# Layer norm sums by halving additions, and modulation pieces moved from the output product to the feed-forward

## The reference, cut to what matters

```python
def layer_norm(x, g, b):
    mu = jnp.mean(xf, axis=-1, keepdims=True)
    var = jnp.mean(jnp.square(xf - mu), axis=-1, keepdims=True)
    y = (xf - mu) * lax.rsqrt(var + LN_EPS)
    return y * g + b

# first block
proj = rms_norm(h, g_mix_pre) @ w_in
attn = moba_attention(q, k, v)                       # 8 heads of 128
conv = silu(layer_norm(depthwise_conv31(glu(u)) + b_dw, ln_g, ln_b))   # 1024 channels
mixed = concatenate([attn, conv], axis=-1) @ w_out   # the output product, 2048 x 2048
h = h + rms_norm(mixed, g_mix_post)
h = h + rms_norm(square(relu(rms_norm(h, g_ffn_pre) @ w_ff1)) @ w_ff2, g_ffn_post)

# second block, in front of each of its two layers, for the vectors c and c_ctx
m = silu(c) @ mod_w + mod_b                          # 2048 x 6144: shift, scale, gate
```

## Time and profile before

| | |
|---|---|
| runs, median of 3 | 1817.17 us (1816.78 to 1817.61) |
| profiled execution | 1817.8 us, its span 1816.1 us |
| TensorE busy | 1795.7 us, 99% |
| VectorE busy | 1472.4 us, 81% |
| ScalarE busy | 903.3 us, 50% |
| GpSimd busy | 113.5 us, 6% |
| DMA | 429.02 MB, mean 236 GB/s |
| 512 KB pieces of `ev_mod_w` | 96 loads, median 5.2 us from issue to landing |

### The profile page before, as it was taken

How to read it: one execution, slowest core, us unless ns; L and a number is a source line. 1 busy time by engine, 2 the same in 40 slices (tenths; PEclk the granted TensorE clock), 3 DMA queues, 4 the chain that set the end, 5 groups by cost and what they waited for, 6 DMA issues and landing times.

```text
span 1816.1 us, 26040 instructions
## 1 busy us (share of the span) xinstructions
PE 1795.7 (99%) x9838; PEld 1553.2 (86%) x9838; DVE 1472.4 (81%) x1712; ACT 903.3 (50%) x1176; POOL 113.5 (6%) x217
## 2 busy tenths in 40 slices
PE   8999999999999999999999999999999999999998
PEld 7899988888888888888888888888888888888986
DVE  6899998878888897889887878765788778897854
ACT  6444566555434433543354557523566546445443
POOL 0000000000000000000000000011111000001000
PEclk9999999999999999999999999999999999999999
DMA  9756447777786787778977966565665784878563
GB/s 324 256 179 192 157 162 291 268 242 265 257 291 228 257 289 233 244 259 295 246 250 267 315 233 235 191 209 164 214 219 191 285 291 130 282 239 283 191 220 105
DMA packets 191304, 429.02 MB, mean 236 GB/s; under 512 B 12512, under 2 KB 12896, under 8 KB 189792
## 3 DMA queue, kind: packets, MB, share of 16 engines
q1 hardware_dynamic: 158560, 323.74, 52.6%
q0 software_dynamic: 27648, 100.68, 16.8%
q10 hardware_dynamic: 4992, 3.16, 0.6%
HBM read 423.33 MB, written 4.21 MB: 235 GB/s over the span
## 4 chain that ended last, share of the span: by engine, by line
PE 94%; DVE 3%; DMA 2%; ACT 1%; issue 1%; SPq 0%; DVEq 0%; ACTq 0%
PE banks L2090 23%; PE banks L2135 14%; PE banks L2137 14%; PE banks L2136 14%; PE banks L2096 12%; PE banks L2081 3%; PE banks L2083 3%; PE banks L2082 3%; PE banks L2446 2%; PE banks L2462 2%; PE banks L2199 1%; PE banks L2437 1%; DVE w_lo L1152 1%; DMA gate_rows<-mod_cols 1%; DMA raw<-in_od_w_out 0%
## 5 line engine op out<-in xcount | busy, mean ns | idle before, releaser
L552 ACT ACTIVATE w_hi<-raw 128x1024 fp32r<-128x1024 f32 x552 | 579.2, 1058 | 648.0 <-PE banks L2137 322.5
L1152 DVE TENSOR_TENSOR w_lo<-raw,w_hi 128x1024 fp32r<-128x1024 f32 x552 | 666.6, 1221 | 229.2 <-ACT w_hi L552 227.0
L2090 PE MATMUL banks<-a_pair,w_hi 128*128 128x512 f32 x1792 | 431.2, 391 | 1.6 <-DVE a_pair L1254 0.9
L2090 PEld LDWEIGHTS banks<-a_pair,w_hi 128*128 128x128 f32 x1792 | 328.4, 188 | 65.2 <-issue 2.2
L2135 PE MATMUL banks<-w_hi,b_hi 128*128 128x512 f32 x808 | 316.2, 391 | 0.2 <-DVE b_lo L1425 0.2
L2137 PE MATMUL banks<-w_hi,b_lo 128*128 128x512 f32 x808 | 314.5, 389 | 0.0
L1192 DVE SCALAR_TENSOR_TENSOR mod_sum<-mod_raw,silu_c,mod_sum 128x1024 f32<-128x1024 f32 x240 | 302.7, 1283 | 14.4 <-DMA mod_raw<-in_od_mod_w 8.1
L2136 PE MATMUL banks<-w_lo,b_hi 128*128 128x512 f32 x808 | 314.4, 389 | 0.0
L2096 PEld LDWEIGHTS banks<-a_pair,w_lo 128*128 128x128 f32 x1792 | 230.2, 191 | 8.8
L2096 PE MATMUL banks<-a_pair,w_lo 128*128 128x256 f32 x1792 | 234.6, 283 | 0.0
L2135 PEld LDWEIGHTS banks<-w_hi,b_hi 128*128 128x128 f32 x808 | 151.7, 188 | 31.9 <-DVE b_lo L1425 0.6
(11 more groups left out here) (249 smaller groups left out, 1679.3 us busy)
## 6 DMA issues: line engine op xcount, KB each, us to landing
raw<-in_w_ff SPq DMA_DIRECT2D x128, 1024.0 KB, 6.7
mod_raw<-in_ev_mod_w POOLq DMA_DIRECT2D x96, 512.0 KB, 5.2
mod_raw<-in_od_mod_w POOLq DMA_DIRECT2D x96, 512.0 KB, 5.7
raw<-in_ev_w_in SPq DMA_DIRECT2D x40, 1024.0 KB, 5.7
raw<-in_w_in SPq DMA_DIRECT2D x39, 1024.0 KB, 5.1
raw<-in_od_w_in SPq DMA_DIRECT2D x32, 1024.0 KB, 6.7
raw<-in_w_out SPq DMA_DIRECT2D x16, 1024.0 KB, 6.3
raw<-in_ev_w_out SPq DMA_DIRECT2D x16, 1024.0 KB, 6.8
```

The costliest lines, as they stand in the source:

```text
L552: nc.scalar.activation(w_hi[:, s % SLOTS], raw[:, s // 2, KPS * (s % 2):KPS * (s % 2) + KPS, :], ACT.Copy).then_inc(hi_ready, 1)
L1152: nc.vector.tensor_tensor(w_lo[:, s % SLOTS], raw[:, s // 2, KPS * (s % 2):KPS * (s % 2) + KPS, :], w_hi[:, s % SLOTS].bitcast(F32), ALU.s ...
L2090: e = nc.tensor.matmul(out[:, f, :], w_hi[:, s % SLOTS, t, P * f:P * (f + 1)], rows[:, :, KPS * s + t, :], start=s == 0 and t == 0, stop=F ...
```

## The change

The layer norm's two sums over the tiles become three halving additions on VectorE (8 tiles to 4, to 2, to 1), the second of them for the squares, in the place of modulation pieces 8 and 9. The eight products with ones for the variance become one, and output step 8 goes ahead of it. VectorE's splits 34 and 35 are each one position earlier in its order. All pieces 8 to 20 leave the output product, and the feed-forward takes 8 to 31 at places 6 to 37 instead of 21 to 31 at places 6 to 27. What follows there (the gate's transposes, then `ev_shift`) starts ten places later and `ev_shift` still ends at place 110.

```diff
+        conv_half = view(R1, CONV_TILES // 2, T)
...
-            nc.vector.tensor_reduce(ln_rstd[:], conv_y.rearrange("p c t -> p t c"), AX.X, ALU.add).then_inc(conv_total, 1)
+            def channels_added(src, done):
+                link(nc.vector.tensor_tensor(conv_half, src[:, 0:4, :], src[:, 4:8, :], ALU.add))
+                link(nc.vector.tensor_tensor(conv_half[:, 0:2, :], conv_half[:, 0:2, :], conv_half[:, 2:4, :], ALU.add))
+                nc.vector.tensor_tensor(ln_rstd[:], conv_half[:, 0, :], conv_half[:, 1, :], ALU.add).then_inc(done, 1)
+            channels_added(conv_y, conv_total)
             ahead1(31)
...
             head_low1(HEADS - 1)
-            halves("ev_gate", 8, 2)
+            dve.wait_ge(conv_sq_ready, 1)
+            channels_added(conv_sq, square_total)
+            ahead1(34)
             dve.wait_ge(ln_sum, 2)
             nc.vector.tensor_scalar(ln_rstd[:], ln_var, 1.0 / 1024, LN_EPS, ALU.mult, ALU.add).then_inc(ln_act, 1)
-            ahead1(34)
+            ahead1(35)
             dve.wait_ge(conv_sq_ready, 2)
...
-            ahead1(35)
             ahead1(36)
...
-            halves("ev_gate", 10, 1)
...
                 for f in range(40 + 4 * i, 44 + 4 * i):
                     ahead1(f)
-                    if f % 2:
-                        halves("ev_gate", 11 + 2 * i + f % 4 // 2, 1)
...
             for f in range(52, 58):
                 ahead1(f)
-                if f < 56:
-                    halves("ev_gate", 17 + f - 52, 1)
...
-                    if 6 <= p < 28:
-                        first, count = spread(p, 6, 28, 11)
-                        halves("ev_gate", 21 + first, count)
-                    elif 28 <= p < 33:
-                        turn("ev_gate", 0, 0, ff_temp, p, 28)
-                    elif 33 <= p < 111:
-                        halves("ev_shift", *spread(p, 33, 111, 32, 3, 4))
+                    if 6 <= p < 38:
+                        first, count = spread(p, 6, 38, 24)
+                        halves("ev_gate", 8 + first, count)
+                    elif 38 <= p < 43:
+                        turn("ev_gate", 0, 0, ff_temp, p, 38)
+                    elif 43 <= p < 111:
+                        halves("ev_shift", *spread(p, 43, 111, 32, 3, 4))
...
-            out_step(6)
-            out_step(7)
-            pe.wait_ge(conv_sq_ready, 1)
+            for n in range(6, 9):
+                out_step(n)
+            pe.wait_ge(square_total, 1)
             pe.wait_ge(head_copied, HEADS)
-            channel_sums(ln_var, conv_sq)
-            for n in range(8, 30):
+            nc.tensor.matmul(ln_var, ones[:], ln_rstd[:], start=True, stop=True).then_inc(ln_sum, 1)
+            for n in range(9, 30):
                 out_step(n)
```

More of the change, by code:

```diff
@@ L295, in build_program @@
         conv_total = sem("conv_total")
+        square_total = sem("square_total")
         conv_sq_ready = sem("conv_sq_ready")
@@ L2322, in head_slot1 @@
                     qkv_step(3 + (6 * m + k) // STEPS, (6 * m + k) % STEPS)
[L2324 to L2328, removed]
             for m in range(HEADS):
```

## The result

The changed kernel takes **1826.28 us** (median of 6 runs, 1824.96 to 1828.55) against 1817.15 us for the kernel before (6 runs, 1816.78 to 1818.30): ratio **1.0051, 95% interval 1.0038 to 1.0064**. It is slower by 9.1 us; 1826.4 us had been forecast. The profiled execution took 1826.65 us with a span of 1825.0 us at a granted clock of 0.999, so the span grew by 8.9 us.

The account below looks back on a forecast made before the run. TensorE, busy 1795.7 of 1816.1 us, was taken to bound the kernel. Median 1817.17 us, with -0.9 for the sums, 0 for pieces leaving the output product and +10.1 for feed-forward stalls, gave 1826.4 us; range 1816.0 to 1834.0.

Parts of the forecast that it names:

- Part 1: Layer-norm sums: TensorE saves 3.02 us, a new 2.0 us wait at output step 12 takes most; -0.9 us.
- The mean's halving: Layer norm: additions take 1.45 us less than the reduction, which only becomes VectorE idle time ahead of line 1456.
- Part 2: Output product: thirteen modulation pieces leave; worth 0, as TensorE did not wait there.
- Part 3: Feed-forward, pieces 9 to 31: TensorE stalls 8 L - 35.5 us, L being issue to landing; at 5.7 us, +10.1 us.
- eight waits of 10 us in sum: Sign in the profile: between 420 and 490 us TensorE waits for w_lo some eight times, up to 2 us each.
- After place 37: Later feed-forward: two-vector pieces at 0.53 instead of 0.46 per step, a buffer having 10 us per two pieces; cost 0.
- A: Feed-forward loads keep up, L at or near the 4.4 us break-even; 1816.3 us; chance 0.26.
- B: Feed-forward loads slow each other, L = 7.5 us gives +24.5, 1840.8 us; chance 0.08.
- C: Step 12 does not wait for conv_ready and loads keep up: full layer-norm gain, -3.0 us, 1814.2 us; chance 0.03.

Follow-up runs that it names:

- e1: Changed layer-norm sums only, against the kernel before; modulation pieces nearly as before (9 to 18 in the output product, 13 in the feed-forward); 1817.38 us, ratio 0.9999.
- e4: Changed kernel, but loads of gate pieces 10 to 31 bring 64 of 1024 columns (32 KB), VectorE's work unchanged; 1816.51 us, ratio 0.9995 to the kernel before.
- e2: Kernel before with its layer norm kept, but pieces 8 to 31 at places 6 to 37 as in the changed kernel; 1827.01 us, ratio 1.0052.
- e6: Changed kernel with pieces 8 to 13 back in the output product's first half and 14 to 31 at feed-forward places 6 to 41; 1817.16 us.
- e8: e6 with the second convolution tile ahead of step 37's rounding and split, and the mean's product ahead of the last head's value product; 1817.05 us.

## Why the prediction was right

*Part 1, TensorE loses 3.02 us and a wait takes 2.0 back (-0.9).* The place of the wait is as read: it is the one of output step 12, on the second convolution tile. It was 1.66 us, not 2.0, and behind it the restart cost more than the 0.1 us I gave it. From 291.15 to 293.20 us and on to 293.54 are 2.39 us for two starts of 0.227: 1.94 us lost where the profile lists 1.66, and 2.1 had been forecast. The saving was 2.85 us, not 3.02: from the last product ahead of the variance's sum to the second behind it are 1.07 us (282.33 to 283.40), against 3.92 before (279.87 to 283.79). So 0.9 it is, by small errors that cancel. The start of the feed-forward moved by 1.12 us with 0.25 of it there already before the layer norm, which is the same 0.9. In the times of whole runs nothing so small is shown by itself (e1 +0.2, e4 -0.6 us in the medians).

*The mean's halving gains nothing.* VectorE's row at 274.56 us (line 1465) is released by the mean's product after 1.43 us of idle time; 1.45 had been forecast. The additions took 1.22, 0.69 and 0.42 us.

*Part 2, the pieces leave the output product, 0.* Right for the change as made. e1 shows that it isn't a law: with TensorE 1 us earlier, ten pieces in that stretch cost 0.6 us at its end. I had read VectorE's reserve there only at the old TensorE's pace.

*Part 3, 8 L - 35.5 us with L = 5.7 (+10.1).* The chain was the right one: piece 9 at 386.97 us and piece 31 at 479.62 us give L = 5.73, and the chain's own eight loads took 5.70 us on average. The formula's lateness is 10.3 us, TensorE's loss 10.7: 0.15 us pass from the split's end to TensorE's start, 0.2 are the earlier trace rows, which is ScalarE's row and not TensorE's, and 0.1 the slower restart. That L came out at 5.7 is partly luck. Choosing the middle between 6.2 and 5.1 was a judgement that no row settled, and its two ends would have given +14.1 and +5.3 us. The eight loads were not alike either (4.0 to 5.0 and 6.6 to 8.0 us), so one L for all of them is an average that happened to fit; in e2 it was 5.65. The forecast of eight waits of 10 us in sum was loose: six, 8.25 us. The other 2.5 us of the 10.7 the list doesn't show. The three waits whose products have rows of their own (2.13, 1.52 and 0.97 us) each cost 0.25 to 0.28 us more than listed, the three others 1.3 us more in sum, and a seventh start, at 462.84 us behind a split that ended at 462.69, came 0.4 us late with no idle time listed. VectorE waited 18.5 us for the loads, some 20 had been forecast.

The Trainium skill's fit for a transfer (DMA: Bandwidth & Descriptors, Anatomy of one DMA), 2.0 us and the bytes over 436 GB/s, had given an estimate of 3.2 us here and so no stall. This case does not agree: the shortest of these loads took 4.0 us in the changed kernel. The half loads (by the fit an estimate of 2.6 us) had a median of 4.1, those of 32 KB (an estimate of 2.1) one of 3.6.

*After place 37, 0.* Right for the changed kernel (0.47 pieces a place). At 0.50 a place, in e6 and e8, a single load of 7.4 us cost a wait of 1.7 us, so the reserve that I had called 10 us per two pieces was thinner than that: VectorE runs ahead in bursts, with one load each 4.66 us (issues at 638.06 and 642.72 us in e8).

The rivals: A (loads keep up) is what e4 shows when the loads are made short, at 1816.5 us against its 1816.3. B and C did not come. The sum: -1.1 + 10.7 is +9.6 behind step 42; 0.6 us come back at 1748 us, and the medians differ by +9.1. +9.2 had been forecast.

## What to carry to other kernels

Work that is moved to where its engine has time still brings its load along. With n buffers and an engine in order, write down the buffer's cycle (work, issue, landing) and count how many cycles the new order chains one behind the other; while every cycle waits for its load, each 1 us of landing is multiplied by that count, so take the landing time from the same stretch, beside the same neighbours, and never from a single transfer. And a gain at one place is only kept if no later place waits for something that does not move with it: follow a landmark (here the start of the second norm) through every variant before calling a local gain worthless.

## What the runs showed of the hardware

- Shortening a load among others buys less than its share of bytes. 512, 256 and 32 KB landed in 5.7, 4.1 and 3.6 us in the median of the same stretch, and at most in 8.0, 6.0 and 4.4 us.
- Loads of one size on one queue can differ by a factor of two by place. The chain's eight loads of 512 KB in the changed kernel landed in 4.0 to 5.0 us where they were issued just ahead of a pair of 1 MB weight loads, and in 6.6 to 8.0 us where they came 1.8 to 2.8 us behind its second. That this order is the reason is not shown.
- A wait costs TensorE more than the listed idle time: products run at 0.227 us a start, their rows last 0.39, and the idle time is counted from the modelled end of the last. With the slower first start behind it, 1.66 us listed were 1.94 lost, and a wait of 0.4 us was not listed at all.
- Halving additions of a contiguous 128x2048 to 128x256 took 2.4 us (1.22 + 0.69 + 0.42 and two steps of 0.03), against 3.85 us for one strided reduction.
